# Attention of a diffusion step: the norm of the prompt's q beside its third product, and adaLN units around the first scores

## What is computed

```python
def qkv_heads(h, wqkv, qn, kn):
    qkv = h @ wqkv                      # 1024 -> 16 q heads, 4 k heads, 4 v heads of 64
    q, k, v = ...
    return rms_norm(q, qn), rms_norm(k, kn), v

# prompt:  softmax(q k^T / 8, with a sink logit) v, keys are the 128 prompt tokens
# latent:  q, k turned by rope2d; keys are the 128 latent tokens and 128 cached ones
# both:    o @ wo, times the adaLN gate, added to y
```

## Time and profile before

| | |
|---|---|
| time, median of 3 runs | 1501.41 us (1499.22 to 1501.93) |
| the profiled execution | 1503.94 us, of which the span is 1502.1 us |
| PE busy | 1417.1 us, 94% |
| DVE busy, ACT busy | 461.5 us, 296.3 us |
| mean PEclk over the span | 0.953 |

### The profile page before, as it was taken

One profiled execution on the slowest core, in us unless ns is written; L12 is line 12 of the kernel. 1 busy time (PEld: TensorE's weight loads), 2 busy tenths in 40 slices (PEclk: granted clock), 3 DMA queues, 4 the chain that ended last, 5 costly groups with the idle time before them and its releaser, 6 DMA issues.

```text
span 1502.1 us, 23843 instructions
## 1 busy us (share of the span) xinstructions
PE 1417.1 (94%) x9546; PEld 843.9 (56%) x9546; DVE 461.5 (31%) x1450; ACT 296.3 (20%) x614; POOL 0.2 (0%) x4
## 2 busy tenths in 40 slices
PE   5798879999999999999988999999999999999996
PEld 2675666555555555555534777655555556555553
DVE  0699361222222222222235223422222222222222
ACT  2301241111111111111132222111111111111111
POOL 0000000000000000000000000000000000000000
PEclk8899889999999999999999559999999999999998
DMA  8989467699999999999992227378999999999980
GB/s 313 373 330 366 162 252 289 245 391 388 412 389 404 401 402 392 401 406 393 415 407 100 104 84 292 150 314 333 386 409 390 408 396 401 400 402 399 403 367 30
DMA packets 80640, 499.45 MB, mean 332 GB/s; under 512 B 10633, under 2 KB 15409, under 8 KB 23760
## 3 DMA queue, kind: packets, MB, share of 16 engines
q1 hardware_dynamic: 80592, 498.79, 82.7%
HBM read 497.45 MB, written 1.31 MB: 332 GB/s over the span
## 4 chain that ended last, share of the span: by engine, by line
PE 89%; DVE 6%; DMA 2%; ACT 1%; issue 1%; SPq 0%; DVEq 0%; ACTq 0%
PE ps L800 31%; PE ps L831 16%; PE ps L781 12%; PE ps L841 9%; PE ps L538 4%; PE ps L584 3%; PE ps L612 3%; PE ps L513 2%; PE ps L678 1%; PE ps L527 1%; DMA ring<-in_conv_w_dram 1%; DVE W L1235 1%; DVE hbf L1235 1%; PE ps L819 1%; PE ps L652 1%
## 5 line engine op out<-in xcount | busy, mean ns | idle before, releaser
L800 PE MATMUL ps<-ring,W 128*64 128x512 f32 x2048 | 453.3, 594 | 1.1 <-ACT W L1094 1.0
L800 PEld LDWEIGHTS ps<-ring,W 128*64 128x64 f32 x2048 | 166.3, 137 | 282.4 <-issue 277.5
L831 PE MATMUL ps<-ring,W 128*64 128x512 f32 x1024 | 233.8, 599 | 1.0 <-DVE W L1486 1.0
L781 PEld LDWEIGHTS ps<-W,hbf 128*128 128x128 bf16 x3168 | 183.1, 98 | 56.4 <-issue 54.2
L781 PE MATMUL ps<-W,hbf 128*128 128x128 bf16 x3168 | 199.1, 219 | 3.0 <-DVE W L1464 2.2
L1492 DVE TENSOR_TENSOR ypart<-ps,ypart 128x512 fp32r<-128x512 f32 x132 | 91.2, 691 | 191.1 <-ACT ypart L1105 191.1
L841 PE MATMUL ps<-comb,ypart 128*128 128x256 f32 x1056 | 141.0, 285 | 2.8 <-DVE ypart L1492 2.8
L1481 DVE SCALAR_TENSOR_TENSOR W<-W,ps 128x256 f32<-128x256 f32 x66 | 31.7, 480 | 351.7 <-ACT W L1099 351.7
L831 PEld LDWEIGHTS ps<-ring,W 128*64 128x64 f32 x1024 | 67.8, 136 | 117.4 <-issue 109.6
L1094 ACT ACTIVATE W<-ps 128x512 f32<-128x512 f32 x132 | 78.8, 597 | 272.5 <-PE ps L781 272.5
L841 PEld LDWEIGHTS ps<-comb,ypart 128*128 128x128 f32 x1056 | 128.8, 188 | 6.2 <-DVE ypart L1492 4.6
(11 more groups left out here) (202 smaller groups left out, 912.5 us busy)
## 6 DMA issues: line engine op xcount, KB each, us to landing
ring<-in_exp_w_gate_dram SPq DMA_DIRECT2D x128, 1024.0 KB, 7.7
ring<-in_exp_w_up_dram SPq DMA_DIRECT2D x128, 1024.0 KB, 10.2
ring<-in_exp_w_down_dram SPq DMA_DIRECT2D x128, 1024.0 KB, 9.6
S<-in_ada_w_dram SPq DMA_DIRECT2D x32, 1024.0 KB, 9.3
ring<-in_ada_w_dram SPq DMA_DIRECT2D x16, 1024.0 KB, 16.1
ring<-in_conv_w_dram SPq DMA_DIRECT2D x4, 2048.0 KB, 19.1
S<-in_attn_wqkv_dram SPq DMA_DIRECT2D x1, 6144.0 KB, 24.4
ring<-in_conv_w_dram SPq DMA_DIRECT2D x1, 4096.0 KB, 20.7
```

The costliest lines, as they stand in the source:

```text
L781: mm = pe.matmul(PG[:, kk * P:(kk + 1) * P], hbf[:, part, g, 4 * half + kk, :], gbf[:, g, :], start=(n == 0), stop=(n == 2 * 3 - 1))
L800: mm = pe.matmul(PGU[64 * b:64 * b + 64, :].rearrange("p (h f) -> p h f", h=2), xg[:, k, 64 * b:64 * b + 64], gate_up_of(w[b])[:, k], star ...
L831: mm = pe.matmul(bank[64 * b:64 * b + 64, :], hidT[:, j, 64 * b:64 * b + 64], down_of(w[b])[:, j, n * 512:(n + 1) * 512], start=(j == 0), ...
```

## The change

DVE norms the prompt's q and k apart. The 16 q heads are done as soon as ACT has copied thirds 0 and 1 (semaphore `at_part` at 5), the 4 k heads after third 2 (at 6). ACT's root of the prompt becomes two, one of 16 columns ahead of the copy of third 2, one of 4 columns where the root stood. The latent's norm is as it was. On PE one unit is put ahead of the first scores and three behind the second ones, where two stood; the loop over heads has units in its first four steps, where it had them in the first six. Semaphore `at_copied`, which counted groups, becomes `at_part`, which counts thirds.

```diff
@@ block.tensor, at_scores
                         if i == 0:
-                            pe.wait_ge(at_copied, 2)
+                            pe.wait_ge(at_part, 6)
@@ block.tensor
                     pe.wait_ge(y_ready, KC)
+                    ada_products(range(EARLY + 8, EARLY + 9), ps[7])
                     at_scores(0)
                     at_scores(1)
-                    ada_products(range(EARLY + 8, EARLY + 10), ps[7])
+                    ada_products(range(EARLY + 9, EARLY + 12), ps[7])
                     for i in range(G * NKV):
                         at_transposes(i)
                         if i + 2 < G * NKV:
                             at_scores(i + 2)
-                        if i < 6:
-                            ada_products([EARLY + 10 + i], ps[7])
+                        if i < 4:
+                            ada_products([EARLY + 12 + i], ps[7])
                         at_values(i)
@@ block.scalar
-                    qkv_copies(1)
-                    qk_roots(1)
-                    qkv_copies(0)
+                    qkv_copies(1, range(3))
+                    qk_roots(1, 20, 40)
+                    qkv_copies(0, range(2))
+                    qk_roots(2, 0, NH)
+                    qkv_copies(0, range(2, 3))
                     act.wait_ge(at_tr, 1)
...
                     qk_copies(1, ps[3:6])
-                    qk_roots(0)
+                    qk_roots(3, NH, 20)
@@ block.vector
+                    def qk_norm(g, n, h0, h1):
+
+                        v = qkv[:, g, h0 * HD:h1 * HD]
+                        v3 = v.rearrange("p (h d) -> p h d", d=HD)
+                        st = stat[:, nqk * g + h0:nqk * g + h1]
+                        sq_g = asq[:, g, h0 * HD:h1 * HD]
+                        step(dve.tensor_tensor(sq_g, v, v, ALU.mult))
+                        dve.tensor_reduce(st, sq_g.rearrange("p (h d) -> p h d", d=HD), AX_X, ALU.add
+                                          ).then_inc(at_qk, 1)
+                        dve.wait_ge(at_root, n)
+                        step(dve.reciprocal(st, st))
+                        step(dve.tensor_tensor(v3, v3, st[:, :, None].to_broadcast([P, h1 - h0, HD]), ALU.mult))
+                        for which, first, last in ((0, 0, NH), (1, NH, nqk)):
+                            f, e = max(first, h0) - h0, min(last, h1) - h0
+                            if f < e:
+                                ins = dve.tensor_tensor(v3[:, f:e, :], v3[:, f:e, :],
+                                                        qkn[:, which:which + 1, :].to_broadcast([P, e - f, HD]),
+                                                        ALU.mult)
+                        return ins
...
                     for g in (1, 0):
-                        dve.wait_ge(at_copied, 2 - g)
-                        if g == 0:
+                        v = qkv[:, g, 0:nqk * HD]
+                        if g == 1:
+                            dve.wait_ge(at_part, 3)
+                            ins = qk_norm(1, 1, 0, nqk)
+                        else:
                             dve.wait_ge(at_nrm, 1)
...
+                            dve.wait_ge(at_part, 5)
+                            qk_norm(0, 2, 0, NH)
+                            dve.wait_ge(at_part, 6)
+                            ins = qk_norm(0, 3, NH, nqk)
```

More of the change, by code:

```diff
@@ L284, in build_kernel @@
         pj_out, pj_bias, pj_done = sem("pj_out"), sem("pj_bias"), sem("pj_done")
-        at_qkv, at_copied, at_qk, at_root, at_nrm, at_tr, at_trc = (
-            sem("at_qkv"), sem("at_copied"), sem("at_qk"), sem("at_root"), sem("at_nrm"), sem("at_tr"), sem("at_trc"))
+        at_qkv, at_part, at_qk, at_root, at_nrm, at_tr, at_trc = (
+            sem("at_qkv"), sem("at_part"), sem("at_qk"), sem("at_root"), sem("at_nrm"), sem("at_tr"), sem("at_trc"))
         at_s, at_max, at_exp, at_pt, at_ptc, at_o, at_on, at_ot, at_otc = (
@@ L1005, in _, with qkv_copies @@
                 else:
-                    def qkv_copies(g):
-                        for n in range(3):
+                    def qkv_copies(g, products):
+                        for n in products:
                             act.wait_ge(at_qkv, 3 * (1 - g) + n + 1)
@@ L1013, in qkv_copies, with qk_roots @@
                                 src = src.rearrange("p (o q d) -> p q o d", o=2, q=QG)
[L1014 to L1019, removed]
+                            act.activation(dst, src, ACT.Copy).then_inc(at_part, 1)
+                    def qk_roots(n, first, last):
+                        act.wait_ge(at_qk, n)
+                        act.activation(stat[:, first:last], stat[:, first:last], ACT.Sqrt,
                                        bias=epsc[:, 0:1], scale=1.0 / HD).then_inc(at_root, 1)
@@ L1269, in _ @@
                     ada_finish(4, ps[2])
-                    for g in (1, 0):
-                        dve.wait_ge(at_copied, 2 - g)
-                        if g == 0:
-                            dve.wait_ge(at_nrm, 1)
[L1274 to L1286, removed]
```

## The result

The changed kernel took 1473.83 us (median of four runs, 1469.93 to 1474.94), the kernel before 1500.32 beside it (1499.16 to 1501.93): a ratio of 0.9819, with a 95% interval of 0.9806 to 0.9831. That is 26.5 us less. The forecast was 1469 with a range of 1463 to 1484. The profiled execution took 1473.77, with a span of 1471.9, which is 30.2 less than the span before.

The account below looks back on a forecast made before the run. PE bounds nearly all; its 4.18 us wait for exponentials also left the head loop at 1.2 GHz. Projection 37 us earlier, less 5 given back, is 32: 1501.4 - 32 = 1469 us, range 1463 to 1484.

Parts of the forecast that it names:

- The norm: DVE's split norm before the heads: q from 808.7 to 814.3, k done at 818.7, first transposes at 823.1 instead of 826.34.
- the wait stays: Rival: q's norm comes too late, PE's wait is 3.3 us and the clock falls as before; 1499.5 us, chance 0.03.
- half of 2.87 later: First scores: one set takes half the pair's 2.87 us, so from 817.36 the first maxima can run at 818.8.
- 37 - 5 = 32: Whole gain in us: output projection 37 earlier through the shorter wait and full-clock loop, less 5 from a late clock fall.
- Clock: Loop over heads: without the long wait, PE's clock stays at 1.00 past 826; up for most or all, chance 0.68.
- the far end of 11 us: Values in the loop: if they did not halve from 3.61 at full clock, 11 us would be lost, giving 1480.
- Given back: Steps 4 to 7: short PE waits make the clock fall about 848 to 857, costing 3 to 7 us, taken as 5.
- PE's waits in the loop at full clock decide: Clock rule for the loop: wait length decides; 1.17 us did not bring a fall, 4.18 did.
- it falls as soon as the loop begins, because this mix can't hold it: Rival: short columns lose the clock at the loop's start; only 3.2 us and 3.7 are won, 1494.5 us, chance 0.09.
- The middle rival: Clock falls at the turning of the prompt's q and k, about 834 to 836; gain 19, time 1482, chance 0.17.
- The base: Starting time: profiled execution 1503.94, median of the runs taken 2.5 lower, so 1501.4 before subtracting the gain.
- The units: adaLN units moved ahead of the loop: two more done by the first transposes, PE's gap there down to some 0.3 us.

Follow-up runs that it names:

- experiment 7: Changed kernel with k heads in the order 0, 2, 1, 3, so steps 0 and 1 use the same 64 array rows: 1471.15 us.
- experiment 8: Kernel before, norm and units untouched, with nine unread matmuls in PE's 4.18 us wait for the exponentials of step 0: 1472.67 us.
- the second execution: Changed kernel profiled again, unaltered, beside the kernel with only the norm split: median 1473.98 us, head stretch 50.84.
- experiment 9: Changed kernel with unread matmuls in PE's short waits before the values of steps 4 to 7 and before the last transposes: 1463.59 us.
- the norm alone: Changed kernel with the norm split but adaLN units where the kernel before had them: 1471.8 us, and 1470.15 when run again.
- experiment 5: Changed kernel with the units of steps 0 to 3 moved: one behind the prompt's q and k turning, three in steps 4 to 6: 1471.05 us.
- experiment 6: Changed kernel with all seven remaining units behind the second scores, none in the loop over heads: 1483.51 us.
- experiment 4: Changed kernel with the three units behind the second scores moved into the loop: four runs of 1472.14 to 1474.33, six of 1493.53 to 1495.33 us.
- experiment 3: Split norm with units at their old places, and the changed kernel again, beside the same runs of the kernel before: 1470.15 and 1473.98 us.
- experiment 10: Split norm with units at their old places, plus unread matmuls in steps 6 and 7 and before the last transposes: 1465.71 us.
- experiment 2: Kernel before with only the units moved to the changed kernel's places, norm in one piece: 1498.02 us, one of ten runs at 1482.38.
- experiment 11: Changed kernel with nine unread matmuls of two columns in a layer 0 wait of PE: 1470.14 us against 1473.98.

## Why the prediction came out right

By its own steps:

**The norm.** DVE on q from 808.7 to 814.3: measured 808.86 to 814.5. The k part's end 818.7: 818.69. First transposes 823.1: 823.34, with a wait of 0.23. Rival "the wait stays" is gone.

**First maxima, 818.9 predicted, 819.46 measured.** The term that failed is "half of 2.87 later": I took one set of scores for half of a pair. Alone it takes 1.92 (the chain of the changed kernel has "824.43 1.92 PE ps L652 x8"), and experiment 7 shows why. The same term runs through the loop: a latent step's 1.44 was 1.92. Steps 0 and 1 took 5.8 and 5.9 and not 5.1 and 5.2, steps 2 and 3 4.9 each and not 4.6 and 4.7. With steps 4 and 5 at 3.5 and 3.4 and not 3.25, the projection started at 867.3 and not at 865. So 37 - 5 = 32 was 29.4. The size of this term was wrong, not the mechanism.

**Clock.** It stayed up past 826, and past the turning of the prompt's q and k (waits 0.59 and 0.89, against 0.6 and 1.0 predicted). Values halved: 1.94 for sixteen in a row, near the 1.80 taken, so the far end of 11 us fell away. This is the larger price of the wait: experiment 8 puts it at 27.1 us, without any work done earlier.

**Given back.** Predicted a fall at 848 to 857 and 5 us: it fell at 856.9, in the second execution at 851.1, and experiment 9 measured 4.0 and 4.95 against these two by taking it away.

**The reason for the clock was only partly right.** "PE's waits in the loop at full clock decide" stood the change and the norm alone, and fell in experiments 5 and 6: waits of 0.64 brought the clock down where the steps had no unit in them, and 1.09 did not where they had. So the work between the waits counts as well. That it came out right in the change is owed to the units in steps 0 to 3, which I had not counted as what holds the clock; that part was luck. What of a unit counts is open: taking one out of a step took its work away and in some steps opened a wait too, and no run separates the two. The rival "it falls as soon as the loop begins, because this mix can't hold it" named the right thing with the wrong verdict: with its units the mix holds the clock, and in experiment 4 it brought it back up; without them it doesn't hold over a wait.

**The middle rival** had the rule that transposes don't count on its side. The change's clock did not fall at the turning. In the change it rose at 867.18, ahead of the projection, with nothing but transposes (L705, L520) on PE since 863.08; in experiment 5 it rose behind ten transposes and one unit (L621, L513), in the kernel before behind L704, L520 and 1.1 us of the projection. None of this sits well with the rule of the Trainium skill, TensorE: Matmul & The Clock Gate, section on PE-mode transpose. These are f32 transposes by an identity. The trace has each of them once (x10 for ten), where it has the other f32 matmuls twice (x18 for the nine of experiment 8), so they do run in another way; whether it is the mode that the section means, no run here shows.

**The base.** I carried 2.5 us from the profiled execution to the median. For the changed kernel the two agree (1473.77, 1473.83). Of the 4.8 us that the forecast was low, 2.5 are that, 2.6 the loop's and 0.4 rounding (1501.4 - 32 is 1469.4), less 0.65 that the last small wait was shorter (4.27 in the change's first trace, 1.65 + 3.27 before). Those 0.65 are chance: the change's second trace has 4.92 there.

**Transfers.** Expert 0's first was issued at 823.17, where 823 was predicted, and PE waits for none ahead of the projection.

**The units** I had counted with the gain. They took the last 0.9 of the wait, which the clock did not need, and left steps 4 and 5 without cover: the change is slower than the norm alone, by 1.9 us in the head stretch of experiment 3. The shortest two are experiment 9 at 1463.6 and experiment 10 at 1465.7; about 3 us of their lead over the change is the last small wait, not the heads.

## What to carry to other kernels

When PE waits some us for other engines in the middle of short work, price the clock of all that follows, not the wait alone: here 4.18 us of wait cost 27 more. Try first what makes the wait short, and if nothing does, fill it with matmuls that nobody reads; and leave real work between short waits rather than move it all ahead of them. When a variant gains more than its place explains, look along the whole trace, since the place of the code alone moved 3.4 us at a far branch.

## What the runs showed of the hardware

A busy PE does not always bring the clock back: with PE busy for 67.42 of 71.5 us it stayed at 1.2 GHz, and in experiment 4 the same kind of loop brought it back after 13.6. Such a program has two times some 20 us apart, each with its own mean clock (six of 54 runs of the kernel before, one of ten in experiment 2, four of ten in experiment 4).

Two sets of eight f32 matmuls (as the trace counts them) of 64 rows and 256 columns took 2.96 us on two halves of the array's rows and 3.72 on one, against 1.92 to 2.00 for a set by itself.

A PE wait "<-issue" behind branches took 4.92 us, and 1.48 when nine small matmuls more (18 in the trace) stood ahead of it. The view of transfers has one instruction transfer inside the wait in the change (1455 to 1459.9) and none in the wait of experiment 11 (1453.3 to 1454.8); it is so in the other traces too, one in each of the ten long waits, none in the four short ones. The Trainium skill, Runtime: NRT & Kernel Launch, section on instruction fetch mechanics, has it that a taken branch to code that isn't held at the time makes the engine wait until it has been fetched; the runs agree in that the code's place matters and that only the long waits hold such a transfer, and don't show which code was held.
